# Two key units of the memory moved between the two norms behind the mixing output

## The chip, the cores and the metric

The kernel runs on one core of a Trainium2 chip. TensorE (PE) multiplies into eight PSUM banks, VectorE (DVE), ScalarE (ACT) and GpSimd (POOL) do the elementwise work, SyncE (SP) issues the weight loads. The metric is the device time of one execution in microseconds (us); lower is better. Everything is computed in f32.

## The reference

Two decoder blocks over 256 tokens of width 2048. What matters here is the end of the first block's mixer, its two norms, and the memory attention of the second block:

```python
mix = (gates[..., :D_MODEL] * (o_a @ w_branch_a[l])
       + gates[..., D_MODEL:] * (o_b @ w_branch_b[l])) @ w_out[l]
x = x + _rmsnorm(mix, g_mix_post[l])
h = _rmsnorm(x, g_ffn_pre[l])
gu = h @ w_ffn_in[l]
...
mix = hybrid_mixer(h, ...)            # S5, stick breaking, sparse attention (16 heads)
...
def memory_cross_attention(h, mem, wq, wkv, wo):
    q = (h @ wq).reshape(bsz, t_len, XA_HEADS, XA_HEAD_DIM)
    k, v = jnp.split(mem @ wkv, 2, axis=-1)
```

`mem` (256 x 2048) is an input, so `mem @ wkv` depends on nothing that the kernel computes and can stand anywhere ahead of the memory attention.

## The kernel before

Activations lie transposed, 128 channels by 256 tokens per block, 16 blocks: `xT` (the residual), `hT` and `yT`, 4096 columns each; everything else shares one scratch tile, `arena`. Every projection is cut into **units** of 256 output columns. A unit's 2 MB of weights come through a ring of four slots; `ORDER` is the list of all units, written out by hand, and the SP queue loads them in this order, the load for a slot when the unit four places ahead has been used (`w_used`). The other engines follow programs of their own and meet through semaphores.

There are two kinds of unit. A plain unit (`unit_quarters`, L598) is 32 matmuls of 128x128 by 256 columns, which the trace writes as 64 records; it is a generator that stops after each quarter (8 matmuls), or after each eighth with `step=4`. A "sevens" unit (`unit_sevens`, L550) does seven of eight block products; for these units POOL first adds blocks of the weights (`sum_weights`, four tensor operations, L517 to L522) and DVE combines blocks of the source (L503 to L510). The mixing output ("out") and the first FFN product ("ffn_in") are of this kind.

The memory's projection is four plain units: `mem_k` 0 and 1 (keys), `mem_v` 0 and 1 (values). Before the change `mem_k` 0 runs behind `ffn_out` while the third norm is worked out, reading the memory from `hT`. The other three run beside the 16 heads of the sparse attention (`nsa_pe`), in eighths, reading the memory from `yT`: one eighth ahead of every head's output product and a second one behind it at even heads, 24 in all.

**Between the two norms.** After the eighth unit of "out", PE adds up the squares of that unit (L758, `norm_sum`). ACT takes the root (L735), DVE the reciprocal (L789), multiplies `yT` by it in four chunks (L805, L809) and adds it to `xT` (L811); ACT squares each chunk (L726); PE sums the squares by 16 matmuls (L742, 32 records); then root, reciprocal, and 16 scalings into `hT` (L798). The first product of "ffn_in" waits for `hT` chunk by chunk (L550); its third product waits for the second of DVE's combinations (L506).

**A head** of the sparse attention: six transposes and two small ones (`turn`, from L2208), ACT copies them to SBUF (L2286, L2288), then the output product on PE (L2222 to L2227), ACT copies the result (L2293) and finishes the next head's exponentials (L2269, L2275), DVE normalizes them (up to L2360), and the next head's `turn` may begin. PE computes the scores two heads ahead (L2195 to L2198) as soon as the bank is free, which is after L2293. At heads 4 and 10 POOL does a weight sum for `out2`.

Of the kernel before, what the change touches and what calls it, by code (L numbers as in the profile page):

```python
# [16 lines left out]
T = 256  # L17
# [55 lines left out]

LATE = [("ng", 0), ("nv", 0), ("nv", 1), ("mem_k", 1), ("mem_v", 0), ("mem_v", 1)]
ORDER = [unit for unit in ORDER if unit not in LATE]
_first = ORDER.index(("out2", 0))
# [158 lines left out]
def build(nc, t_in, t_out):  # L235

    ctx = ExitStack()
    with ctx:
# [65 lines left out]
        def stream_weights(sp):  # L304
            for n, home in enumerate(LOADS):
                if n >= RING:
                    sp.wait_ge(w_used, n - RING + 1)
                if isinstance(home, int):
                    sp.dma_start(ring[:, n % RING, :], weights[home, :, :]).then_inc(w_ready[n % RING], 16)
                else:  # L310
                    for half in range(2):
                        q, (a, z) = (home[1] + half) // 3, PAIRS[(home[1] + half) % 3]
                        for row in range(2):
                            to = 2048 * half + 256 * (z - a) * row
                            sp.dma_start(ring[:, n % RING, to:to + 256 * (z - a)],
                                         weights[home[0] + 2 * q + row, :, 256 * a:256 * z])\
                                .then_inc((w_late if half else w_ready)[n % RING], 16)
                if n == UNIT_AT["branch_b0", 0][0] + RING - 1:
                    gate_loads(sp)
                if n == UNIT_AT["mem_k", 1][0]:  # L320
                    nsa_loads(sp)
# [3 lines left out]
        def run(steps):  # L325
            for _ in steps:
                pass
# [378 lines left out]

        NORM_AT = {"mix_post": 0, "ffn_pre": 0}
        POST = {"out": ("norm_units", 0), "ffn_out": ("norm_units", 8), "out2": ("ln_units", 0), "down2": ("ln_units", 8)}

        def norm_space(tag):  # L710
            sq, r = carve(DB * T, T, at=NORM_AT.get(tag, 11264))
            return sq.rearrange("p (b t) -> p b t", b=DB), r

# [30 lines left out]

        def unit_sums(pe, name, src, done):

# [16 lines left out]
            def after(u):  # L763
                released = u // per_slot * per_slot
                for v in range(max(0, released - per_slot), released) if u % per_slot == 0 else ():
                    add(v)
                if u == st.units - 1:
                    for v in range(released, st.units):
                        last = add(v)
                    last.then_inc(sem(done), 1)  # L770
# [776 lines left out]
        bb_combined = combined_in_place(obT, arena[:, 16400:17424], arena[:, 17424:18448], arena[:, 0:1024])  # L1547
        out_combined = combined_in_place(mixT, *carve(1024, 1024, 1024, at=4352))
        out_squares = carve(512, at=7424)[0].rearrange("p (h t) -> p h t", h=2)
        bb_temps = carve(P, T, at=18448)  # L1550
# [21 lines left out]
        def gates_pool(pool):  # L1572
            pool.wait_ge(sem("rw2_Y_sum"), RW_TILES // GT * NCH)
            summed = [("branch_b", u) for u in range(7)] + [("out", u) for u in range(8)]
            for n, (name, u) in enumerate(summed):
# [5 lines left out]
                if n == 4:  # L1581
                    nsa_consts_pool(pool)

        def branch_b_pe(pe):
# [3 lines left out]

        def out_pe(pe):
            short_pe(pe, "out", mixT, lambda u: bb_sums[u % 2], out_combined, "mix_ready", 1,  # L1590
                     unit_sums(pe, "out", out_squares, "norm_sum"))

# [110 lines left out]
        def ffn_dve(dve):  # L1703
# [3 lines left out]
            for u in range(st.units):  # L1707
                left, right, first, u2 = ffn_out_of[u % 2]
                if u == st.units - 1:
                    out_stage_idle(dve, "mem_k")  # L1710
                    sum_weights(dve, "ffn_out", 0, 0, fo_sums[0])
                    group_used(dve, "ffn_in", u - 1, 0)
                    sum_weights(dve, "ffn_out", 0, 1, fo_sums[1])
# [435 lines left out]
        def nsa_pe(pe):  # L2149
# [82 lines left out]
            for h in range(NH):  # L2232
# [3 lines left out]
                if h == 0:  # L2236
                    pe.wait_ge(sem("mem_loaded"), 32)
                next(memory, None)
                output(h)
                if h % 2 == 0:  # L2240
                    next(memory, None)
            run(memory)
            pe.wait_ge(sem("attn_head_done"), NSA_AT_HEAD + NH)

        def nsa_act(act):
# [34 lines left out]
            for h in range(NH):  # L2280
# [13 lines left out]
                if h + 1 < NH:  # L2294
                    exponentials(h + 1, 1)
                if h in (5, 11):
                    store_unit(act, *LATE[3 + h // 6])
            store_unit(act, *LATE[5])

# [377 lines left out]
        def _(pe):  # L2677
# [14 lines left out]
            out_pe(pe)  # L2692
            squares_pe(pe, "ffn_pre", pm[0])
            ffn_pe(pe)
            ffn_out_pe(pe)
            pe.wait_ge(sem("mem_loaded"), 16)
            run(unit_quarters(pe, "mem_k", 0, hT))
            products(pe, "u5", xT, ready="block1_done", count=NCK, chunks=NCK)
# [10 lines left out]
        def _(act):  # L2709
# [16 lines left out]
            root_act(act, "mix_post", pm[0], 0)  # L2726
            squares_act(act, "ffn_pre", xT, "x_mixed", NCK)
            root_act(act, "ffn_pre", pm[0], 0)
            ffn_act(act)
            root_table_act(act)  # L2730
            ffn_out_act(act)
            root_act(act, "ffn_post", pm[0], 0)
            store_unit(act, "mem_k", 0)
            s5_angles_act(act)
# [188 lines left out]
```

## Time and profile before

| | us |
|---|---|
| median of 3 runs | 4033.61 |
| lowest, highest | 4032.55, 4039.31 |
| the profiled execution | 4030.8 |
| its span in the trace | 4028.9 |
| PE busy in it | 3857.7 (96%) |
| POOL busy in it | 1241.4 (31%) |

The span is what the trace covers, from the first to the last instruction. PE is busy almost throughout, so the places that count are those at which PE waits, and those at which it works at a lower granted clock. The profile gives the granted clock as a share of full speed: 1.00 is 2.4 GHz, 0.50 is 1.2 GHz.

### The profile page before, as it was taken

The page shows a single profiled execution, that of the slowest core. Times are in us where ns is not written, and L with a number is a line of the kernel's source. Part 1 is how long each engine was busy: PE and PEld are TensorE (multiplying, and loading weights), DVE is VectorE, ACT ScalarE, POOL GpSimd, SP SyncE. Part 2 cuts the span into 40 slices and gives each one's busy share as a digit, 9 for nine tenths or more (in the row PEclk, how much of TensorE's full clock was granted, in tenths as well). Part 3 has the DMA queues.
Part 4 walks back from the last instruction along what each step waited for, and adds up shares of the span by engine and source line. Part 5 has one row for each costly group of instructions (what it writes and reads, how often), then busy time and mean ns, then how long its engine had stood idle before and what let it go on. Part 6 is the DMA issues. An engine that isn't in the chain of part 4 may idle for free.

```text
span 4028.9 us, 65270 instructions
## 1 busy us (share of the span) xinstructions
PE 3857.7 (96%) x28244; PEld 3561.4 (88%) x28244; DVE 1769.7 (44%) x3203; ACT 600.3 (15%) x1315; POOL 1241.4 (31%) x783
## 2 busy tenths in 40 slices
PE   8999999999999999999999999997798899999997
PEld 7888888888788998999999998776597899999997
DVE  1344425540313513111144455723422688887544
ACT  0333311111111011000000000222302211111001
POOL 0000000003222774777740000001150477775000
PEclk9999999999999999999999999998899999999999
DMA  6566654456654443444444554354142344444442
GB/s 239 195 225 225 220 207 170 160 191 215 194 179 159 155 168 110 170 170 171 170 158 160 172 206 170 140 128 158 45 160 97 115 168 168 168 168 163 167 158 79
DMA packets 109118, 668.81 MB, mean 166 GB/s; under 512 B 23056, under 2 KB 27472, under 8 KB 78496
## 3 DMA queue, kind: packets, MB, share of 16 engines
q1 hardware_dynamic: 64208, 549.01, 37.6%
q0 software_dynamic: 21088, 69.73, 5.8%
q10 hardware_dynamic: 23536, 45.92, 3.2%
q8 instruction: 222, 3.64, 0.4%
q14 instruction: 64, 0.52, 0.0%
HBM read 611.34 MB, written 53.25 MB: 165 GB/s over the span
## 4 chain that ended last, share of the span: by engine, by line
PE 89%; DVE 4%; issue 3%; ACT 2%; POOL 1%; POOLq 1%; DVEq 1%; ACTq 1%; DMA 0%
PE product_bank L550 46%; PE product_bank L598 31%; PE product_bank L392 3%; PE mixer_bank L742 1%; PE mixer_bank L758 1%; POOL arena L519 1%; POOLq L521 1%; POOLq L518 0%; POOL arena L522 0%; ACT xT L859 0%; PE mixer_bank L1271 0%; PE mixer_bank L1285 0%; PE mixer_bank L1122 0%; ACTq L2276 0%; DVE arena L1357 0%
## 5 line engine op out<-in xcount | busy, mean ns | idle before, releaser
L598 PE MATMUL product_bank<-hT,weight_ring 128*128 128x256 f32 x3648 | 812.4, 381 | 0.0
L598 PEld LDWEIGHTS product_bank<-hT,weight_ring 128*128 128x128 f32 x3648 | 689.5, 190 | 103.2 <-issue 10.2
L550 PE MATMUL product_bank<-hT,weight_ring 128*128 128x128 f32 x3680 | 457.6, 277 | 14.1 <-DVEq L1628 5.8
L550 PEld LDWEIGHTS product_bank<-hT,weight_ring 128*128 128x128 f32 x3680 | 435.8, 193 | 16.7 <-issue 6.8
L550 PE MATMUL product_bank<-arena,weight_ring 128*128 128x128 f32 x3200 | 398.5, 275 | 0.0
L550 PEld LDWEIGHTS product_bank<-arena,weight_ring 128*128 128x128 f32 x3200 | 378.5, 192 | 0.6
L517 POOL TENSOR_TENSOR arena<-weight_ring 128x1024 f32<-128x1024 f32 x89 | 212.8, 2391 | 479.5 <-PE product_bank L550 307.7
L574 DVE TENSOR_TENSOR arena<-product_bank,arena 128x128 f32<-128x128 f32 x127 | 36.9, 290 | 730.9 <-PE product_bank L550 730.9
L2601 DVE SCALAR_TENSOR_TENSOR arena<-arena 128x256 f32<-128x256 f32 x176 | 322.4, 1870 | 14.2 <-ACT arena L2566 10.9
L520 POOL TENSOR_TENSOR weight_ring<-weight_ring 128x1024 f32<-128x1024 f32 x111 | 272.1, 2452 | 0.0
L550 PE MATMUL product_bank<-hT,arena 128*128 128x128 f32 x2048 | 250.9, 277 | 0.2 <-DVE hT L506 0.2
L550 PEld LDWEIGHTS product_bank<-hT,arena 128*128 128x128 f32 x2048 | 240.9, 194 | 0.6 <-DVE hT L506 0.6
L519 POOL TENSOR_TENSOR arena<-arena,weight_ring 128x1024 f32<-128x1024 f32 x89 | 212.2, 2385 | 34.2 <-issue 22.6
L522 POOL TENSOR_TENSOR arena<-arena,weight_ring 128x1024 f32<-128x1024 f32 x89 | 212.0, 2382 | 12.9 <-issue 0.4
L550 PE MATMUL product_bank<-yT,weight_ring 128*128 128x128 f32 x1632 | 199.9, 276 | 6.9 <-POOL arena L522 6.9
L550 PE MATMUL product_bank<-yT,arena 128*128 128x128 f32 x1632 | 198.6, 276 | 0.0
L550 PEld LDWEIGHTS product_bank<-yT,weight_ring 128*128 128x128 f32 x1632 | 191.2, 193 | 7.5 <-issue 7.5
L550 PEld LDWEIGHTS product_bank<-yT,arena 128*128 128x128 f32 x1632 | 190.8, 193 | 0.0
L550 PE MATMUL product_bank<-xT,weight_ring 128*128 128x128 f32 x1408 | 174.5, 277 | 8.0 <-ACT xT L859 8.0
L550 PEld LDWEIGHTS product_bank<-xT,weight_ring 128*128 128x128 f32 x1408 | 166.1, 193 | 9.3 <-issue 6.2
L598 PE MATMUL product_bank<-xT,weight_ring 128*128 128x256 f32 x768 | 170.7, 380 | 0.6 <-PE mixer_bank L1941 0.2
L564 ACT ACTIVATE arena<-product_bank 128x128 f32<-128x128 f32 x127 | 34.4, 271 | 875.2 <-PE product_bank L550 864.0
(495 smaller groups left out, 5353.3 us busy)
## 6 DMA issues: line engine op xcount, KB each, us to landing
weight_ring<-in_weights SPq DMA_DIRECT2D x213, 2048.0 KB, 8.0
weight_ring<-in_weights SPq DMA_DIRECT2D x128, 512.0 KB, 5.6
weight_ring<-in_weights SPq DMA_DIRECT2D x64, 384.0 KB, 5.8
units<-out_stage ACTq DMA_DIRECT2D x87, 256.0 KB, 7.8
rwkv_keep<-arena ACTq DMA_DIRECT2D x16, 1282.0 KB, 6.1
arena<-rwkv_keep POOLq DMA_DIRECT2D x8, 1280.0 KB, 7.3
arena<-units POOLq DMA_DIRECT2D x36, 256.0 KB, 3.4
arena<-units POOLq DMA_DIRECT2D x48, 128.0 KB, 6.0
```

Source lines behind the costliest of these rows:

```text
L392: mm = pe.matmul(out, lhs, rhs, start=first, stop=kk == slots * st.blocks - 1, skip_group_check=slots > 1)
L517: eng.tensor_tensor(s1, B11, B12, ALU.add)
L519: eng.tensor_tensor(s2, s1, B22, ALU.add)
L520: eng.tensor_tensor(B12, B12, B22, ALU.add)
L521: eng.drain()
L522: eng.tensor_tensor(s4, s2, B21, ALU.add).then_inc(sem(f"weights_summed_by_{SUMMED_BY[name]}"), 1)
L550: mm = pe.matmul(bank[:, at * P:at * P + P], lhs[:, j, :], rhs[:, j, :], start=g == 0 and n in (0, 3) and j == 0, stop=g == n_groups - 1 a ...
L574: dve.tensor_tensor(u2, X[:, P:2 * P], first, ALU.add)
L598: mm = pe.matmul(psg[b][:, half * T:half * T + T], lhs, rhs, start=k == 0, stop=k == 15)
L742: mm = pe.matmul(bank[:, 0:T], const("ones_mean"), sq[:, b, :], start=b == 0, stop=b == DB - 1)
L758: mm = pe.matmul(pm[0][:, 0:T], const("ones_mean"), v, start=n == 0, stop=n == DB - 1)
L2601: last = dve.scalar_tensor_tensor(V[:, h, :], U[:, h, k:k + T], col(h, k), V[:, h, :], ALU.mult, ALU.add)
```

## The change

Both key units go between the norms. `mem_k` 0 and 1 stand ahead of `ffn_in` in `ORDER`. PE runs one quarter of `mem_k` 0 between the squares' sum of the seventh and of the eighth unit of "out", its three others behind the eighth's, then two quarters of `mem_k` 1, the sum of squares of the second norm, and the last two quarters. POOL loads the memory into `arena` for it (`early_mem`, 2 MB), in its queue behind the weight sum for "out" 1. `mem_v` 0 takes `mem_k` 0's place behind `ffn_out`. Only `mem_v` 1 remains beside the heads, one eighth ahead of the output product of every even head. Scratch places in `arena` move so that nothing overlaps. Around the change only the order and the places differ; the work is the same, but for one more load of the memory.

```diff
-LATE = [("ng", 0), ("nv", 0), ("nv", 1), ("mem_k", 1), ("mem_v", 0), ("mem_v", 1)]
-ORDER = [unit for unit in ORDER if unit not in LATE]
+LATE = [("ng", 0), ("nv", 0), ("nv", 1), ("mem_v", 1)]
+EARLY = [("mem_k", 0), ("mem_k", 1)]
+ORDER = [unit for unit in ORDER if unit not in LATE + EARLY]
+_first = ORDER.index(("ffn_in", 0))
+ORDER[_first:_first] = EARLY
...
                 if u == st.units - 1:
+                    run(filler)
                     for v in range(released, st.units):
                         last = add(v)
                     last.then_inc(sem(done), 1)
...
+                if n == 8:
+                    pool.wait_ge(sem("mix_ready"), 1)
+                    pool.dma_start(early_mem, t_in["memT"]).then_inc(sem("mem_loaded"), 16)
...
         def out_pe(pe):
+            first = unit_quarters(pe, "mem_k", 0, early_mem)
+            def part(n):
+                pe.wait_ge(sem("mem_loaded"), 16)
+                for _ in range(n):
+                    next(first)
+                    yield
             short_pe(pe, "out", mixT, lambda u: bb_sums[u % 2], out_combined, "mix_ready", 1,
-                     unit_sums(pe, "out", out_squares, "norm_sum"))
+                     unit_sums(pe, "out", out_squares, "norm_sum", part(1)))
+            run(first)
+
+        def between_norms_pe(pe):
+            second = unit_quarters(pe, "mem_k", 1, early_mem)
+            next(second)
+            next(second)
+            squares_pe(pe, "ffn_pre", pm[0])
+            run(second)
...
-                next(memory, None)
-                output(h)
                 if h % 2 == 0:
                     next(memory, None)
+                output(h)
             run(memory)
...
-            squares_pe(pe, "ffn_pre", pm[0])
+            between_norms_pe(pe)
             ffn_pe(pe)
             ffn_out_pe(pe)
-            pe.wait_ge(sem("mem_loaded"), 16)
-            run(unit_quarters(pe, "mem_k", 0, hT))
+            pe.wait_ge(sem("mem_loaded"), 32)
+            run(unit_quarters(pe, "mem_v", 0, hT))
...
             squares_act(act, "ffn_pre", xT, "x_mixed", NCK)
+            store_unit(act, "mem_k", 0)
             root_act(act, "ffn_pre", pm[0], 0)
+            store_unit(act, "mem_k", 1)
             ffn_act(act)
```

PE's queue from the end of the last "out" unit to the start of "ffn_in", before (a row is one line of instructions with its count of matmuls; L758 and L742 are the two sums of squares):

```order
L550 MATMUL product_bank<-arena 128x128 x8
L550 MATMUL product_bank<-arena,weight_ring 128x128 x8
L758 MATMUL mixer_bank<-arena,consts 128x256 x4
L742 MATMUL mixer_bank<-arena,consts 128x256 x16
L550 MATMUL product_bank<-hT,weight_ring 128x128 x8
L550 MATMUL product_bank<-hT,arena 128x128 x8
```

and after the change, with the lines moved on by 4 to 7 (L765 and L749 are the sums, L602 is the plain unit):

```order
L554 MATMUL product_bank<-arena 128x128 x8
L554 MATMUL product_bank<-arena,weight_ring 128x128 x8
L765 MATMUL mixer_bank<-arena,consts 128x256 x2
L602 MATMUL product_bank<-arena,weight_ring 128x256 x8
L765 MATMUL mixer_bank<-arena,consts 128x256 x2
L602 MATMUL product_bank<-arena,weight_ring 128x256 x40
L749 MATMUL mixer_bank<-arena,consts 128x256 x16
L602 MATMUL product_bank<-arena,weight_ring 128x256 x16
L554 MATMUL product_bank<-hT,weight_ring 128x128 x8
L554 MATMUL product_bank<-hT,arena 128x128 x8
```

The eighth unit's sum stands behind a quarter of `mem_k` 0; 40 matmuls stand ahead of the second norm's sum and 16 behind it.

PE's queue beside the heads, at the end of an even head's `turn` (L2212), before; L598 is an eighth of a memory unit, L2222 to L2227 the output product, L2195 the scores of the head after next:

```order
L2210 MATMUL mixer_bank<-consts,arena 128x128
L2212 MATMUL mixer_bank<-consts,arena 15x128 x2
L598 MATMUL product_bank<-weight_ring,yT 128x256 x4
L2222 MATMUL mixer_bank<-arena 64x256
L2226 MATMUL mixer_bank<-arena 64x256
L2227 MATMUL mixer_bank<-arena 64x128
L2226 MATMUL mixer_bank<-arena 64x256
L2227 MATMUL mixer_bank<-arena 64x128
L598 MATMUL product_bank<-weight_ring,yT 128x256 x4
L2195 MATMUL mixer_bank<-arena 128x256
L2196 MATMUL mixer_bank<-arena 128x128
L2195 MATMUL mixer_bank<-arena 128x256
```

and after, at an odd head's `turn` (L2240), where the output product is L2250 to L2255 and the scores L2223 and L2224:

```order
L2238 MATMUL mixer_bank<-consts,arena 128x128
L2240 MATMUL mixer_bank<-consts,arena 15x128 x2
L2250 MATMUL mixer_bank<-arena 64x256
L2254 MATMUL mixer_bank<-arena 64x256
L2255 MATMUL mixer_bank<-arena 64x128
L2254 MATMUL mixer_bank<-arena 64x256
L2255 MATMUL mixer_bank<-arena 64x128
L2223 MATMUL mixer_bank<-arena 128x256
L2224 MATMUL mixer_bank<-arena 128x128
L2223 MATMUL mixer_bank<-arena 128x256
```

At even heads the first eighth stays where it was and the second is gone; at odd heads no eighth is left.

## Rows read from the trace of the kernel before

**Rows 1.** windows of core 0 from the last mixing product to the FFN
```profile
core 0: us, PE busy (x) PEld busy (x) DVE busy (x) ACT busy (x) POOL busy (x), PEclk, DMA share, GB/s
1503.30:1514.17 10.87, 2.13 (x10) 1.22 (x8) 8.01 (x10) 3.07 (x5) 5.95 (x3) 0.79 0.51 193
1514.17:1524.16 9.99, 9.95 (x32) 7.97 (x32) 4.81 (x4) 3.17 (x4) 0.00 (x0) 0.72 0.00 0
...
1528.32:1537.05 8.73, 7.72 (x31) 6.83 (x32) 8.45 (x16) 0.00 (x0) 0.00 (x0) 0.51 0.00 0
```

**Rows 2.** timeline of PE there: start us, us, instructions [idle before <-releaser]
```profile
1505.87 1.13 PE L758 MATMUL mixer_bank<-arena,consts 128*128 128x256 f32 x4 [1.57 <-ACT arena L780]
1514.17 9.95 PE L742 MATMUL mixer_bank<-arena,consts 128*128 128x256 f32 x32 [7.17 <-ACT arena L726]
1528.32 1.20 PE L550 MATMUL product_bank<-hT,weight_ring 128*128 128x128 f32 x4 [4.20 <-DVE hT L798]
...
1533.99 3.33 PE L550 MATMUL product_bank<-hT,arena 128*128 128x128 f32 x16
1537.16 1.95 PE L550 MATMUL product_bank<-yT,arena 128*128 128x128 f32 x16
```

**Rows 3.** timeline of ACT and DVE there
```profile
1509.37 1.22 DVE L805 TENSOR_TENSOR yT<-yT,arena 128x1024 f32<-128x1024 f32 x1
...
1519.25 1.06 ACT L726 ACTIVATE arena<-xT 128x1024 f32<-128x1024 f32 x1 [0.26 <-DVE xT L811]
1524.16 0.47 ACT L735 ACTIVATE arena<-mixer_bank,small 128x256 f32<-128x256 f32 x1 [3.86 <-PE mixer_bank L742]
...
1526.50 6.42 DVE L798 SCALAR_TENSOR_TENSOR hT<-xT,params,arena 128x256 f32<-128x256 f32 x16
...
1534.15 1.22 DVE L506 TENSOR_TENSOR yT<-hT 128x1024 f32<-128x1024 f32 x1
```

**Rows 4.** timeline of PE behind the FFN, one whole memory unit
```profile
2370.04 13.98 PE L598 MATMUL product_bank<-hT,weight_ring 128*128 128x256 f32 x64
```

**Rows 5.** timeline of POOL and DVE at the start of the mixing output
```profile
1394.98 3.18 DVE L503 TENSOR_TENSOR arena<-hT 128x1024 f32<-128x1024 f32 x1
1397.22 3.15 POOL L522 TENSOR_TENSOR arena<-arena,weight_ring 128x1024 f32<-128x1024 f32 x1
```

**Rows 6.** DMA issues from 1440 us to 1560 us: count, KB each, median us to landing
```profile
weight_ring<-in_weights SPq DMA_DIRECT2D x7, 2048.0 KB, 7.8
```

**Rows 7.** timeline of the SP queue around the end of "out" 6: start us, us to the last issue
```profile
1490.09 13.70 SPq L309 DMA_DIRECT2D weight_ring<-in_weights  x2
```

**Rows 8.** windows of the heads: all, three intervals, one with a POOL sum; columns as [rows 1]
```profile
2757.67:2928.32 170.65, 133.79 (x648) 100.59 (x648) 86.65 (x345) 60.11 (x231) 32.38 (x34) 0.89 0.20 69
2796.39:2805.80 9.41, 6.77 (x38) 5.10 (x38) 5.02 (x24) 3.90 (x15) 1.06 (x2) 1.00 0.08 21
2805.80:2817.10 11.30, 10.30 (x46) 7.63 (x46) 5.03 (x24) 3.80 (x15) 1.06 (x2) 0.85 0.26 65
...
2826.51:2837.47 10.96, 10.30 (x46) 7.72 (x47) 5.02 (x24) 3.80 (x15) 1.06 (x2) 0.84 0.07 18
...
2769.54:2784.77 15.23, 6.77 (x38) 5.09 (x39) 11.57 (x24) 3.91 (x15) 10.35 (x6) 0.82 0.03 6
```

**Rows 9.** waits of PE beside the heads: us in total, times, longest
```profile
PE mixer_bank L2208 <- DVE arena L2360: 41.2, 16, 8.0
```

**Rows 10.** windows of the heads, the memory units' products alone
```profile
2757.67:2928.32 170.65, 55.35 (x192) 41.76 (x192) 0.89 0.20 69
```

**Rows 11.** timeline of one odd and one even head
```profile
2798.28 0.41 ACT L2288 ACTIVATE arena<-mixer_bank 15x128 f32<-15x128 f32 x2
...
2799.15 0.64 PE L2222 MATMUL mixer_bank<-arena 15*64 15x256 f32 x2
...
2805.80 0.33 PE L2208 MATMUL mixer_bank<-consts,arena 128*128 128x128 f32 x1 [2.17 <-DVE arena L2360]
...
2806.80 3.50 PE L598 MATMUL product_bank<-yT,weight_ring 128*128 128x256 f32 x8
```

More of the change, by code:

```diff
@@ L319, in stream_weights @@
                     gate_loads(sp)
-                if n == UNIT_AT["mem_k", 1][0]:
+                if n == UNIT_AT["mem_v", 1][0]:
                     nsa_loads(sp)
@@ L707, in build @@
         NORM_AT = {"mix_post": 0, "ffn_pre": 0}
+        ROOT_AT = {"mix_post": 17920, "ffn_pre": 17920}
         POST = {"out": ("norm_units", 0), "ffn_out": ("norm_units", 8), "out2": ("ln_units", 0), "down2": ("ln_units", 8)}
@@ L711, in norm_space @@
             sq, r = carve(DB * T, T, at=NORM_AT.get(tag, 11264))
+            if tag in ROOT_AT:
+                r, = carve(T, at=ROOT_AT[tag])
             return sq.rearrange("p (b t) -> p b t", b=DB), r
@@ L743, in squares_pe, with unit_sums @@
             mm.then_inc(sem("norm_sum"), 1)
-        def unit_sums(pe, name, src, done):
+        def unit_sums(pe, name, src, done, filler=()):
             st = PLAN[name]
@@ L1547, in build @@
         bb_combined = combined_in_place(obT, arena[:, 16400:17424], arena[:, 17424:18448], arena[:, 0:1024])
-        out_combined = combined_in_place(mixT, *carve(1024, 1024, 1024, at=4352))
-        out_squares = carve(512, at=7424)[0].rearrange("p (h t) -> p h t", h=2)
+        out_combined = combined_in_place(mixT, *carve(1024, 1024, 1024, at=4096))
+        early_mem = arena[:, 7168:7168 + 4096].rearrange("p (b t) -> p b t", b=DB)
+        out_squares = carve(512, at=17408)[0].rearrange("p (h t) -> p h t", h=2)
         bb_temps = carve(P, T, at=18448)
@@ L1709, in ffn_dve @@
                 if u == st.units - 1:
-                    out_stage_idle(dve, "mem_k")
+                    out_stage_idle(dve, "mem_v")
                     sum_weights(dve, "ffn_out", 0, 0, fo_sums[0])
@@ L2236, in nsa_pe @@
                 if h == 0:
-                    pe.wait_ge(sem("mem_loaded"), 32)
-                next(memory, None)
-                output(h)
+                    pe.wait_ge(sem("mem_loaded"), 48)
                 if h % 2 == 0:
                     next(memory, None)
+                output(h)
             run(memory)
@@ L2295, in nsa_act @@
                     exponentials(h + 1, 1)
-                if h in (5, 11):
-                    store_unit(act, *LATE[3 + h // 6])
-            store_unit(act, *LATE[5])
+            store_unit(act, *LATE[3])
         def nsa_dve(dve):
@@ L2732, in _ @@
             root_act(act, "ffn_post", pm[0], 0)
-            store_unit(act, "mem_k", 0)
+            store_unit(act, "mem_v", 0)
             s5_angles_act(act)
```

## The prediction

> **What bounds the kernel now.** I first read the page: PE is busy 96% of the span, so a move of PE work pays only where it fills a wait of PE or ends a slow clock, and costs where the place it leaves had hidden it. Then the windows and timelines of both places.
>
> Between the norms PE has nothing to do three times: 1.57 us ahead of the eighth unit's sum, 7.17 us ahead of the second norm's, 4.20 us ahead of "ffn_in" [rows 2]. The granted clock goes with it: the sum of squares that follows the long wait gets 0.72 and takes 9.95 us, and "ffn_in" starts at 0.51, which is 1.2 GHz nearly throughout [rows 1]. The reader should see a chain of ACT and DVE (root, reciprocal, multiply, add, square, [rows 3]) that PE waits out. This place can swallow work.
>
> Beside the heads PE waits too, 41.2 us over 16 heads, always for DVE's last normalization [rows 9], though 24 eighths of memory units, 55.35 us of PE, lie there [rows 10]. So the eighths don't bound the heads, but the loop PE, ACT, PE, ACT, DVE does. An odd interval (an eighth ahead of the output, none behind) takes 9.41 us at clock 1.00; an even one, with two eighths, 11.30 or 10.96 us at 0.85 or 0.84 [rows 8]. Where does the difference come from? The second eighth runs while ACT and DVE work, and DVE releases the odd `turn` behind it too (16 of 16). The difference is the clock: ahead of the even `turn` PE idles 2.17 us, and right behind it the eighth takes 3.50 us for 8 records [rows 11], against 13.98 / 8 = 1.75 us by the whole unit [rows 4]. 1.75 of the 1.89 us difference is this one eighth.
>
> **The change, part by part.**
>
> *PE between the norms.* A quarter of a unit is 13.98 / 4 = 3.5 us at full clock [rows 4]. The seventh unit's sum starts at 1503.3 and takes about 0.9 us. Then:
> - the first quarter ends at 1507.6, and the eighth unit's sum starts there and not at 1505.87 [rows 2]: the norm chain is 1.75 us late, and the last square (1519.25 + 1.06 = 1520.3 before, [rows 3]) at 1522.1;
> - sum to 1508.5, five quarters, 17.5 us, to 1526.0;
> - the second norm's sum, 32 records, costs two quarters' worth at full clock, 7.0 us, to 1533.0, instead of 1524.1;
> - the last two quarters to 1540.0. Meanwhile root, reciprocal and scalings: before, from L735 at 1524.16 to the end of L798 at 1532.92 are 8.8 us, and to the end of L506 at 1535.37 are 11.2 us [rows 3]. So `hT` is whole at 1541.8 and the third product of "ffn_in" may start at 1544.2. It started at 1537.16 [rows 2], held by the slow clock (the second product took 3.33 us).
>
> That makes +7.0 us for 28.0 us of work: 21 us are hidden. PE is late by its own work up to 1540, then DVE for 2 us.
>
> *POOL and SP.* Two loads now stand ahead of "ffn_in" in the SP queue, so the weights for "ffn_in" 0 are asked for when "out" 6 is done (1490) and for 1 when "out" 7 is (1503), the two issues of [rows 7], and land 7.8 us later [rows 6]. POOL sums them, some 10.35 us each [rows 8], from about 1498 and 1511, needed at 1540 and later: no wait. But the second sum now runs on top of DVE's ten-odd us of norm work. Where the two engines met before, DVE's L503 took 3.18 us beside a POOL operation of 3.15 us [rows 5]; the same shape alone takes 1.22 us [rows 3]. Four POOL operations cost DVE about 4 x 2.0 = 8 us: the last square comes at 1530.1, and PE wants it at 1526.0 + 3/4 of 7.0 = 1531.3. So I take 0, with 1.2 us to spare: the cover is `mem_k`'s quarters. Without that cover it is up to +8.
>
> The Trainium skill, page GPSIMD Engine Reference, section 1. Specifications, has this as a rule against the change: GpSimd's SBUF interfaces are shared with VectorE, with contention for DVE instructions with two SBUF inputs, as L805 to L811 are. The trace agrees (3.18 against 1.22 us). By that rule alone nothing of the sum changes while the cover holds.
>
> *The other queues.* POOL's load of the memory waits for `mix_ready` behind the sum for "out" 1, which ends at 1400.4 [rows 5]; behind it stands the sum for "out" 2, which waits for PE anyway. 100 us lie before its use. ACT's two copies of `mem_k` are one activation each, under the 1.06 us of L726 [rows 3], behind which the second root waits for PE. "mem_v" 0 costs behind the FFN what `mem_k` 0 did [rows 4]. All 0. Lower bound for the whole place +6 (DVE's last 2 us overlap better), upper +12 (half of the contention uncovered).
>
> *The heads.* 16 eighths go, 16/24 of 55.35 = 37 us of PE. At odd heads the output may start when ACT's copies are done (2798.28 + 0.41 = 2798.7) and not at 2799.15 [rows 11]: -0.4 us, at six of eight, since at two the POOL sum sets the pace (15.23 us, POOL 10.35, [rows 8]): -2. At even heads the eighth behind the output was hidden: 0. What is left is the clock. The eighth that filled the time ahead of every odd `turn` is gone, so that PE now idles over 2 us ahead of every `turn`, not of every second one. Bounds from rows: never a fall of the clock, even intervals 9.41 instead of 11.30 or 10.96 us, eight times -1.6, with the -2 makes -15. A fall at every head: odd intervals lose what their output product loses at half clock, at most the 1.75 us of an eighth (nearly as many columns), so about +1.3 net at six, +8, and +12 if it outlasts one head. Falls as often as now: -2. A wait that makes the clock fall at even heads should do so at some odd heads, not all, since an even interval lost 1.89 us and another 1.55 [rows 8], and heads differ: I take the middle of -2 and +10, **+4**.
>
> The Trainium skill, page TensorE: Matmul & The Clock Gate, section What's actually happening, says that the throttled state is the default and activity releases it. By that a thinner stage is slower: the case of +8 to +12. The trace agrees in kind: the intervals at 1.00 are those that follow the filled wait [rows 8].
>
> *Sum.* Against the profiled execution's 4030.8 us (span 4028.9): +7 + 4 = 4042. The median of the runs is 2.8 us above it, so 4033.6 + 11 = **4045**.
>
> **The rivals.** Differences under 0.2%, 8.1 us, can't be told from none here.
> 1. *Forecast*: norms +7, heads 0 to +12: 4041 to 4053. Chance 0.53.
> 2. *The clock falls beside the heads as often as now*: 7 - 2, 4039. For it: one fall a pair is regular; against: the waits double. 0.20.
> 3. *The clock stays up beside the heads*: 7 - 15, 4026, just within 0.2%. Against: every long wait of [rows 11] is followed by a slow stretch. 0.08.
> 4. *The heads shorten by what leaves them* (the other side): if the eighths sat on the loop, -37, so 4033.6 + 7 - 37 = 4004. It decides once the heads give back over 15 us (7 + 8.1), and wants the output product and `turn` to wait for PE's own queue; [rows 9] show DVE as releaser 16 times of 16. 0.05.
> 5. *Contention uncovered*: both POOL sums on the norm chain, twice 8 us against 9.2 us of cover, so about +7 more with the heads at +4: 4052. 0.14.
>
> **How the numbers follow.** Likeliest 4045. Range 4034 to 4056: it leaves out 3 and 4 (0.13) and the far tail of 5 and of slow heads. The forecast's own range is 4041 to 4053. Slower by over 0.2% (from 4041.7): most of 1, all of 5: 0.64. Within: the rest of 1, 2, most of 3: 0.29. Faster: 4 and a bit of 3: 0.07.
>
> **What would show it.** In the profile after: PE busy without a wait from the last "out" product to "ffn_in", clock 1.00 there; the second norm's sum about 7 us long; "ffn_in"'s third product 40 to 42 us after the seventh unit's sum (34 before); DVE multiplications of over 3 us instead of 1.22. Beside the heads: odd intervals with clock below 1.00, the 16 heads 170.65 + 4 us, PE's waits up from 41 to 70 us or more. Wrong if odd intervals keep 1.00 (then 2 or 3), or if PE waits for a square (then 5).

## The result: 0.6% slower, and outside the range

| | before | after |
|---|---|---|
| median, us | 4033.08 (4 runs) | 4060.32 (4 runs) |
| lowest, highest | 4031.74, 4039.31 | 4058.56, 4063.30 |
| the profiled execution | 4030.8 | 4061.84 |
| heads, first `turn` to the first product of "out2" | 171.9 | 191.0 |

The ratio is 1.0063, 95% interval 1.0047 to 1.0079. The forecast was 4045, with a range up to 4056: the sign was right, the size was not. The page of the changed kernel, its span and PE's busy time:

```profile
span 4060.0 us, 65273 instructions
PE 3884.3 (96%) x28244; PEld 3578.2 (88%) x28244; DVE 1775.4 (44%) x3203; ACT 600.1 (15%) x1315; POOL 1244.7 (31%) x784
```

PE has the same 28244 records as before, yet is busy 26.6 us longer (3857.7 before). The same matmuls took longer, so the clock comes first, and waits second. I laid the two PE timelines over each other, instruction by instruction, and noted by how much the changed kernel was behind. This gives four steps:

| place | behind by | grown there |
|---|---|---|
| third product of "ffn_in" | 6.9 us | +6.9 |
| `turn` of the first head | 9.1 us | +2.2 |
| first product of "out2" | 28.1 us | +19.1 |
| behind "out2", in the memory attention | 31.2 us | +3.1 |

The two spans differ by 31.1 us (4060.0 - 4028.9), so nothing is missing. (The difference of the medians is 27.2: the profiled execution of after was 1.5 us above its median, that of before 2.3 below.)

**Between the norms** everything is as forecast. PE's timeline of the changed kernel:

```profile
1504.06 3.62 PE L602 MATMUL product_bank<-arena,weight_ring 128*128 128x256 f32 x16
1507.51 1.03 PE L765 MATMUL mixer_bank<-arena,consts 128*128 128x256 f32 x4
1508.38 17.43 PE L602 MATMUL product_bank<-arena,weight_ring 128*128 128x256 f32 x80
1525.64 7.07 PE L749 MATMUL mixer_bank<-arena,consts 128*128 128x256 f32 x32
1532.55 7.07 PE L602 MATMUL product_bank<-arena,weight_ring 128*128 128x256 f32 x32
1539.46 1.50 PE L554 MATMUL product_bank<-hT,weight_ring 128*128 128x128 f32 x12
1541.57 0.71 PE L554 MATMUL product_bank<-hT,weight_ring 128*128 128x128 f32 x4 [0.61 <-DVE hT L806]
...
1544.02 1.16 PE L554 MATMUL product_bank<-yT,arena 128*128 128x128 f32 x8
```

Against [rows 2] the three waits (1.57, 7.17, 4.20 us) are gone, the second norm's sum takes 7.07 us instead of 9.95, and one wait of 0.61 us for `hT` is left. The third product starts 6.9 us later (1537.16 before); the sum had +7.0. On the timelines of DVE and POOL the contention is there, and PE does not see it:

```profile
1512.06 3.37 DVE L817 TENSOR_TENSOR yT<-yT,arena 128x1024 f32<-128x1024 f32 x1
1515.51 3.22 DVE L819 TENSOR_TENSOR xT<-xT,yT 128x1024 f32<-128x1024 f32 x1
...
1511.14 3.21 POOL L521 TENSOR_TENSOR arena<-weight_ring 128x1024 f32<-128x1024 f32 x1 [3.72 <-DMA weight_ring<-in_weights]
...
1529.10 1.06 ACT L733 ACTIVATE arena<-xT 128x1024 f32<-128x1024 f32 x1 [0.26 <-DVE xT L819]
```

**Beside the heads** the windows of the changed kernel (columns as [rows 1]; the whole stretch, an odd and an even interval in its first half, an odd and an even one in its second):

```profile
2766.73:2957.69 190.96, 137.74 (x520) 95.90 (x521) 84.11 (x346) 59.88 (x231) 32.42 (x34) 0.67 0.13 45
2830.09:2841.50 11.41, 7.49 (x30) 4.79 (x31) 5.03 (x24) 3.91 (x15) 1.06 (x2) 0.66 0.07 19
2841.50:2853.65 12.15, 9.64 (x39) 6.95 (x39) 5.02 (x24) 3.80 (x15) 1.06 (x2) 0.75 0.07 16
...
2879.07:2890.74 11.67, 9.42 (x30) 6.46 (x30) 5.03 (x24) 3.91 (x15) 1.06 (x2) 0.50 0.07 18
2890.74:2902.22 11.48, 8.97 (x39) 6.82 (x39) 5.02 (x24) 3.80 (x15) 1.06 (x2) 0.80 0.06 17
```

In an odd interval DVE, ACT and POOL are busy as long as in [rows 8] (5.03, 3.91 and 1.06 us against 5.02, 3.90 and 1.06). What changed is the clock: 0.67 over the stretch instead of 0.89, and 0.50, which is 1.2 GHz from end to end, in the odd intervals of the second half, but for the last head. PE has 128 fewer records there than before (520 against 648) and is busy longer, 137.7 us against 133.8. Its waits:

```profile
PE mixer_bank L2236 <- DVE arena L2385: 42.9, 16, 7.6
PE mixer_bank L2250 <- ACTq L2316: 10.2, 8, 1.3
PE mixer_bank L2223 <- ACT hT L2320: 6.5, 14, 0.5
```

The wait for DVE hardly grew (41.2 in [rows 9]; the prediction looked for 70 or more), since slow PE work now fills the time in which fast PE work would have left it idle. New is the second row: with no eighth ahead of it, the odd output product waits for ACT's copies. One such odd head on PE's timeline:

```profile
2879.07 0.47 PE L2236 MATMUL mixer_bank<-consts,arena 128*128 128x128 f32 x1 [2.41 <-DVE arena L2385]
...
2882.32 1.11 PE L2250 MATMUL mixer_bank<-arena 15*64 15x256 f32 x2 [1.27 <-ACTq L2316]
2883.36 1.12 PE L2254 MATMUL mixer_bank<-arena 128*64 128x256 f32 x2
...
2886.65 1.22 PE L2223 MATMUL mixer_bank<-arena 64*128 64x256 f32 x2 [0.47 <-ACT hT L2320]
```

From `turn` to the output product are 3.25 us, against 2.76 in [rows 11] (2796.39 to 2799.15), where an eighth lay in between. From the start of the output product to ACT's copy of it (L2320) are 3.90 us, against 2.13 before, and from there to the next `turn` 4.52 us in both. The transposes, the output product and the scores all run at half speed, and the first two are on the loop.

### The profile page after: what moved, and what is told of

It reads as the page before. It is cut to its first block, busy times and chain, and to the rows that moved or that the text cites. A ratio compares the mean times of both kernels' runs of the same rounds, so it can differ in the third digit from the quotient of the medians.

```text
span 4060.0 us, 65273 instructions
## 1 busy us (share of the span) xinstructions
PE 3884.3 (96%) x28244; PEld 3578.2 (88%) x28244; DVE 1775.4 (44%) x3203; ACT 600.1 (15%) x1315; POOL 1244.7 (31%) x784
## 4 chain that ended last, share of the span: by engine, by line
PE 89%; DVE 3%; issue 3%; ACT 2%; POOL 1%; POOLq 1%; DVEq 1%; ACTq 1%; DMA 0%
PE product_bank L554 45%; PE product_bank L602 31%; PE product_bank L396 3%; PE mixer_bank L749 1%; PE mixer_bank L765 1%; POOL arena L523 1%; POOLq L525 1%; POOLq L522 0%; POOL arena L526 0%; ACT xT L867 0%; PE mixer_bank L2254 0%; PE mixer_bank L1279 0%; PE mixer_bank L1293 0%; PE mixer_bank L1130 0%; ACTq L2303 0%
## 5 line engine op out<-in xcount | busy, mean ns | idle before, releaser
L602 PE MATMUL product_bank<-hT,weight_ring 128*128 128x256 f32 x3584 | 798.4, 381 | 0.0
L602 PEld LDWEIGHTS product_bank<-hT,weight_ring 128*128 128x128 f32 x3584 | 677.3, 190 | 101.5 <-issue 10.2
L554 PEld LDWEIGHTS product_bank<-hT,weight_ring 128*128 128x128 f32 x3680 | 435.2, 193 | 12.7 <-DVEq L1656 6.0
L554 PEld LDWEIGHTS product_bank<-xT,weight_ring 128*128 128x128 f32 x1408 | 166.2, 193 | 9.3 <-issue 6.2
L602 PE MATMUL product_bank<-xT,weight_ring 128*128 128x256 f32 x768 | 172.4, 383 | 0.6
L602 PEld LDWEIGHTS product_bank<-xT,weight_ring 128*128 128x128 f32 x768 | 146.2, 192 | 22.3 <-issue 2.1
```

The costliest lines, as they stand in the source:

```text
L554: mm = pe.matmul(bank[:, at * P:at * P + P], lhs[:, j, :], rhs[:, j, :], start=g == 0 and n in (0, 3) and j == 0, stop=g == n_groups - 1 a ...
L602: mm = pe.matmul(psg[b][:, half * T:half * T + T], lhs, rhs, start=k == 0, stop=k == 15)
```

## The experiments

None of the kernels leaves out work. "Idle" matmuls are added work whose result nobody reads. A "group" is four matmuls of 128x128 by 256 columns, an eighth of a memory unit or idle work of that size. The table orders the kernels by their groups beside the heads; "heads" is the time from the first `turn` to the first product of "out2" in the profiled execution. Each ratio is to runs of the kernel before that were taken together with the kernel's own, whose medians were 4032.0 to 4033.8 us.

| kernel | groups ahead of / behind the output | heads, us | median, us | ratio to before |
|---|---|---|---|---|
| after | 8 / 0 | 191.0 | 4060.3 | 1.0063 |
| `e8_pool_later` | 8 / 0 | 191.0 | 4059.7 | 1.0067 |
| `e7_idle_ahead` | 16 / 0 | 187.2 | 4059.6 | 1.0061 |
| `e10_half_idle` | 8 and 8 half / 8 half | 178.6 | 4051.8 | 1.0048 |
| `e4_one_between` | 0 / 16 | 176.9 | 4038.9 | 1.0012 |
| before | 16 / 8 | 171.9 | 4033.1 | |
| `e1_idle_as_before` | 16 / 8 | 171.9 | 4042.8 | 1.0025 |
| `e2_idle_behind` | 8 / 16 | 172.3 | 4044.0 | 1.0024 |
| `e3_behind` | 8 / 16 | 173.4 | 4035.4 | 1.0003 |
| `e5_filled` | 16 / 16 | 166.0 | 4029.2 | 0.9986 |
| `e6_filled_norms` | 16 / 16, and idle work between the norms | 166.6 | 4030.7 | 0.9993 |
| `e9_filled_long` | 16 / 16 and long waits | 162.5 | 4025.3 | 0.9975 |

**Idle work in the old places.** My theory after the result: the 19 us are the clock, and the clock fell because work was taken from PE.

```diff
+            def idle_work():
+                for k in range(4):
+                    pe.matmul(psg[(spare + 1) % 4][:, 0:T], xT[:, k, 0:P], yT[:, k, :], start=k == 0, stop=k == 3)
...
                 if h % 2 == 0:
                     next(memory, None)
+                else:
+                    idle_work()
                 output(h)
+                if h % 2 == 0:
+                    idle_work()
```

> The changed kernel with idle matmuls beside the sparse attention's heads: four matmuls of 128x128 by 256 columns, as long as an eighth of a memory unit, into a product bank whose contents nobody reads, at each of the 16 places where the kernel before had an eighth and the changed one has none (ahead of the output at odd heads, behind it at even ones). They add computation and no loads. Theory A, the 19 us that the heads grew by are the lower clock and nothing else of the move: with PE's old load back the 16 heads take 171 us again instead of 191, the granted clock there is back near 0.89, PE's waits for DVE are back near 41 us, and the total is 4033 + 7 (norms) + 2 (the stretch ahead of the heads) = 4042, though PE does 37 us more of work than in the changed kernel. Theory B, the heads grew for another reason (their exponentials, the weight loads or POOL's sums now fall elsewhere): the total stays at 4060 and the heads at 190 us. Theory C, work on PE is what bounds the heads: the added 37 us make it slower, up to 4097.

4042.84 us, ratio 1.0025 (1.0015 to 1.0034). The windows of the heads, of an odd and of an even one:

```profile
2766.44:2938.32 171.88, 133.77 (x648) 100.60 (x649) 87.52 (x346) 59.95 (x231) 32.39 (x34) 0.89 0.15 51
2805.17:2814.58 9.41, 6.77 (x38) 5.10 (x38) 5.02 (x24) 3.91 (x15) 1.06 (x2) 1.00 0.08 21
2814.58:2825.89 11.31, 10.30 (x47) 7.62 (x47) 5.03 (x24) 3.80 (x15) 1.06 (x2) 0.85 0.08 20
```

The two intervals are those of [rows 8] again, to 0.01 us, and the stretch takes the 171.9 us of the kernel before. PE got 16 groups of work that is good for nothing, and the median fell by 17.5 us from that of the changed kernel (4060.3). Theory A holds; loads, POOL and DVE's contention have no part in the 19 us.

**Does the place of a group matter?** Three kernels ask it from different sides. First the changed kernel with the idle groups behind the output at every head:

```diff
                 output(h)
+                idle_work()
```

> The changed kernel with the same idle group of four matmuls behind the output product of every head, odd ones too, and none ahead of it; the eighth of the value unit stays ahead of the output at even heads. The same 16 groups as in the kernel with idle work at the old places, but eight of them stand where PE waits for DVE and not where ACT and DVE wait for PE. Theory A, the clock follows how long PE stands still ahead of each turn: with an eighth behind every output no wait is over 1 us, the granted clock stays at 1.00, odd and even intervals take 9.4 us as the odd ones of the kernel before, the heads come to about 155 us, and the total to 4060 - 36 = 4025. Theory B, the clock follows only how much work there is in all, not its place: as with the old places, 4042. Theory C, the place behind the output is no cover, since DVE's normalization is done by then: each head grows by up to 1.75 us, above 4060.

Second the kernel before with its own eighths in that order:

```diff
-                next(memory, None)
-                output(h)
                 if h % 2 == 0:
                     next(memory, None)
+                output(h)
+                next(memory, None)
```

> The kernel before, with its 24 eighths of memory units in another order beside the heads: behind the output product at every head, and ahead of it only at even heads (before: ahead of it at every head, behind it only at even ones). Everything else, the norms too, is as before. Theory A (waits ahead of turn set the clock): all intervals at 9.4 us, heads 155 us instead of 171, total 4033 - 16 = 4017. Theory B (only the amount of PE work counts): no difference from the kernel before, 4033 within 4 us.

4044.0 (1.0024, 1.0013 to 1.0034) and 4035.4 (1.0003, 0.9993 to 1.0012): both theories A are wrong. With 24 groups the order makes no difference to the total that can be measured, though it changes which intervals are slow. Windows of the heads of `e3_behind`, and of three intervals, two odd ones with an even one behind the second:

```profile
2757.89:2931.24 173.35, 143.49 (x648) 103.71 (x649) 89.29 (x348) 61.16 (x233) 32.38 (x34) 0.85 0.18 65
...
2816.09:2825.12 9.03, 6.97 (x38) 5.09 (x38) 5.03 (x24) 4.51 (x16) 1.06 (x2) 1.00 0.55 228
2859.32:2870.60 11.28, 10.00 (x38) 6.82 (x39) 4.98 (x23) 3.92 (x15) 1.06 (x2) 0.70 0.06 18
2870.60:2879.88 9.28, 8.63 (x48) 6.53 (x47) 5.19 (x24) 3.80 (x15) 1.06 (x2) 1.00 0.64 233
```

and the two odd heads on PE's timeline, the first in the interval at 1.00 and the second in the one at 0.70:

```profile
2816.09 0.33 PE L2208 MATMUL mixer_bank<-consts,arena 128*128 128x128 f32 x1 [1.00 <-DVE arena L2360]
2818.46 0.64 PE L2222 MATMUL mixer_bank<-arena 15*64 15x256 f32 x2 [1.28 <-ACTq L2289]
...
2859.32 0.33 PE L2208 MATMUL mixer_bank<-consts,arena 128*128 128x128 f32 x1 [1.01 <-DVE arena L2360]
2861.70 1.11 PE L2222 MATMUL mixer_bank<-arena 15*64 15x256 f32 x2 [1.28 <-ACTq L2289]
```

Both have the same two waits; in the one the output product ran at full clock (0.64 us), in the other at half (1.11 us). So waits of 1.0 and 1.3 us can be enough for a fall, and need not be. At full clock and with no eighth ahead of it, the output product starts 2.37 us behind `turn`, and the interval is 9.03 us instead of 9.41.

Third the changed kernel with idle groups ahead of the output at odd heads alone:

```diff
                 if h % 2 == 0:
                     next(memory, None)
+                else:
+                    idle_work()
                 output(h)
```

> The changed kernel with 8 idle groups beside the heads, all ahead of the output product of odd heads, so that one eighth or its like stands ahead of every output and none behind: half of what the change took away. Theory A (the wait of over 2 us ahead of a turn brings the slow stretch; filling only the far side of the output leaves a 2.17 us wait ahead of every turn): heads stay above 185 us, total 4056 or more. Theory B (the clock follows the amount of work in the heads, in proportion): halfway between 171 and 191, so heads 181 us and total 4050. Theory C (one group a head is enough, as it was with the groups behind the output): heads 172 us, total 4042.

4059.55 us (1.0061), heads 187.2 us: the times are theory A's, and B and C are out. PE still stands still for 2.04 us or more ahead of every `turn`. Sixteen groups all ahead of the output give 187.2 us, sixteen all behind it (`e4_one_between`, below) 176.9. So the place matters, below 24 groups. The windows of the heads, first of `e7_idle_ahead`, then of `e4_one_between`, show that it doesn't act through the share of slow time:

```profile
2766.96:2954.17 187.21, 136.80 (x584) 101.13 (x585) 84.91 (x346) 59.89 (x231) 32.41 (x34) 0.78 0.13 47
...
2758.44:2935.35 176.91, 138.57 (x584) 95.42 (x585) 89.99 (x348) 60.55 (x232) 32.39 (x34) 0.78 0.15 51
```

The mean clock is 0.78 in both. What differs is what runs slowly. In `e7_idle_ahead` the group ahead of the output is on the loop at half clock, and from `turn` to the output product are 4.1 to 5.3 us at every head; in `e4_one_between` 2.37 us, or 3.25 where `turn` itself is slow.

**A third arrangement of the same work.** One key unit between the norms, the other back beside the heads, an eighth behind each output (the diff is against the changed kernel).

```diff
-LATE = [("ng", 0), ("nv", 0), ("nv", 1), ("mem_v", 1)]
-EARLY = [("mem_k", 0), ("mem_k", 1)]
+LATE = [("ng", 0), ("nv", 0), ("nv", 1), ("mem_k", 1), ("mem_v", 1)]
+EARLY = [("mem_k", 0)]
...
-            run(first)
+            next(first)
+            next(first)
+            squares_pe(pe, "ffn_pre", pm[0])
+            run(first)
...
-                if h % 2 == 0:
-                    next(memory, None)
                 output(h)
+                next(memory, None)
```

> The same work as before and after, in a third arrangement: only the first key unit between the norms (one quarter between the two sums of squares of the mixing output, two ahead of the second norm's sum, one behind it), the second key unit and the second value unit beside the heads with one eighth behind the output product of every head and none ahead, the first value unit behind the FFN. Theory A (one hidden eighth per head keeps the clock up): heads 155 to 158 us, the norms within 2 us of the kernel before, total 4033 - 15 = 4018. Theory B (16 eighths are too few for the clock wherever they stand): heads at 180 us or more, total 4040 or more. Theory C (the clock stays at the old share): 171 us, total 4032.

4038.9 us (1.0012, 1.0002 to 1.0021), heads 176.9 us: none of the three; the total is nearest to B's. PE's timeline between the norms:

```profile
1503.88 1.03 PE L765 MATMUL mixer_bank<-arena,consts 128*128 128x256 f32 x4
1504.74 3.62 PE L602 MATMUL product_bank<-arena,weight_ring 128*128 128x256 f32 x16
...
1509.06 7.07 PE L602 MATMUL product_bank<-arena,weight_ring 128*128 128x256 f32 x32
...
1537.80 1.96 PE L554 MATMUL product_bank<-yT,arena 128*128 128x128 f32 x16
```

From the seventh unit's sum to the third product are 33.9 us, as in [rows 2] (1503.3 to 1537.16) without any of `mem_k` there. The first unit between the norms is free there, and the second one costs the 7 us. But even the free place gains nothing: the heads, with 16 groups left, took 5.0 us more than before.

**Filling the heads.** Now the kernel before with an idle group behind odd outputs too, so that only waits of 0.65 to 1.0 us are left ahead of most `turn`s.

```diff
                 output(h)
                 if h % 2 == 0:
                     next(memory, None)
+                else:
+                    idle_work()
```

> The kernel before with an idle group of four matmuls (128x128 by 256 columns, a result that nobody reads) behind the output product of every odd head, so that an eighth or its like stands ahead of and behind every output: 32 instead of 24. It adds 8 x 1.75 = 14 us of PE work and changes nothing else. Theory A (a slow stretch needs a wait of some length on PE; the ones that were left when the eighths stood behind every output were 1.28 us ahead of odd outputs and 1.0 ahead of turns, and that was still enough): here only the waits of 0.65 to 1.0 us ahead of turn are left, the granted clock stays at 1.00, intervals are 9.4 to 9.6 us, the heads take 157 us instead of 171, and the total is 4032 - 14 = 4018. Theory B (the slow stretch comes once in two heads whatever stands there, as in the four kernels with 16 or 24 groups): heads 171 us, total 4032. Theory C (the added work lengthens the loop): above 4035.

4029.24 us, ratio 0.9986 (0.9978 to 0.9995): 14 us more of PE work, and faster. The windows of the heads, an odd and an even one:

```profile
2759.68:2925.64 165.96, 142.06 (x713) 107.32 (x714) 88.03 (x347) 61.49 (x234) 32.41 (x34) 0.92 0.21 73
2798.46:2807.88 9.42, 8.63 (x47) 6.54 (x47) 5.04 (x24) 3.91 (x15) 1.06 (x2) 1.00 0.08 21
2807.88:2817.50 9.62, 8.62 (x47) 6.53 (x47) 5.03 (x24) 3.80 (x15) 1.06 (x2) 1.00 0.29 70
```

Theory A in direction, under half of it by size (5.9 of 14 us in the heads): five even intervals fell from 10.8 to 11.3 us to 9.3 to 9.6, which is 8.2 us, but the last head took 2.2 us more. I had counted eight. Whether it was the shorter waits or the larger amount of work that kept the clock up, this kernel can't tell, since it changes both; `e3_behind` had waits of 1.0 us too, with less work, and lost the clock behind some of them.

Then the long waits as well:

```diff
+                for k in range({0: 16, 2: 13, 8: 9}.get(h, 0)):
...
+                    pe.matmul(psg[(spare + 1) % 4][:, 0:T], xT[:, k % 4, 0:P], yT[:, k % 4, :], start=True, stop=True)
                 turn(h)
```

> The kernel with 32 groups beside the heads (24 eighths of memory units and 8 idle groups, which ran in 4029), with idle matmuls also in the three long waits that were left there: 16 ahead of the first head's turn, 13 ahead of the third's, 9 ahead of the ninth's (0.44 us each at full clock, in waits of 7.6, 6.6 and 4.8 us). Theory A (a slow stretch follows a long wait, and costs up to 2 us an interval): the intervals behind them fall from 11.9, 11.6 and 11.3 us to 9.4 to 9.6, those with a POOL sum stay at 13.4 to 15.2, which POOL sets; the heads take 160 us instead of 166, total 4029 - 6 = 4023. Theory B (these intervals are slow because POOL's sum slows DVE in them, not by PE's clock): no change, 4029.

4025.32 us, ratio 0.9975 (0.9966 to 0.9984), 8.5 us below the kernel before in the runs taken with it (4033.8): the fastest of all. The windows of its heads and of the first three intervals:

```profile
2758.66:2921.20 162.54, 147.34 (x756) 111.84 (x757) 89.29 (x347) 61.42 (x234) 32.43 (x34) 0.98 0.21 75
2758.66:2768.30 9.64, 8.62 (x47) 6.53 (x47) 5.04 (x24) 3.80 (x15) 1.06 (x2) 1.00 1.00 423
2768.30:2784.70 16.40, 14.43 (x73) 11.39 (x73) 12.84 (x24) 3.91 (x15) 10.37 (x6) 1.00 0.03 9
2784.70:2793.97 9.27, 8.62 (x46) 6.53 (x47) 5.02 (x24) 3.80 (x15) 1.06 (x2) 1.00 0.13 36
```

Theory A, and B is out: 11.9 us became 9.64 and 11.6 became 9.27, and the ninth interval, not shown, 9.65 instead of 11.30. But the interval with POOL's sum took 16.40 instead of 15.24, and the tenth one fell to 0.85 and took 1.7 us more, so 3.4 of the 6 us came.

**Half the amount.** The first experiment again, with

```diff
-                for k in range(4):
+                for k in range(2):
```

> The changed kernel with idle groups at the 16 old places of the eighths, as in the run that took 4043, but of two matmuls instead of four: half of the PE work that the change took from the heads. Theory A (with so much the slow stretch still ends in time, since a group stands on both sides of each output): heads 175 us or less, total 4046 or less. Theory B (in proportion to the work): heads 181 us, total 4051. Theory C (half-filled waits count as unfilled): heads 187 us or more, total 4056 or more.

4051.84 us (1.0048), heads 178.6 us: between A and B by the heads. Half of the work gives back 12.4 of the 19.1 us there.

**Contention.**

```diff
                 if u == 1:
+                    pool.wait_ge(sem("norm_squares"), SQUARES_AT["ffn_pre"] + NCK)
                 sum_weights(pool, "ffn_in", u, 0, ffn_sums[u % 2])
```

> The changed kernel, in which POOL's weight sum for the second unit of the first FFN product waits until ACT has squared the last chunk of the second norm. In the changed kernel that sum runs on top of DVE's four norm operations, which take 3.2 to 3.4 us each instead of 1.22. Theory A (the prediction's: contention is covered by the quarters of the second key unit): DVE's operations take 1.22 us again, the last square comes near 1522 instead of 1530, PE does not notice, and the total is 4060 within 2 us. Theory B (part of the 7 us lost between the norms, or of the 27 us in all, is this contention, for instance through hT, which is needed at 1540): up to 4 us faster, 4056. Theory C (the sum comes too late for its unit): slower, by up to 6 us, with a wait of PE for POOL.

4059.72 us (1.0067): theory A. DVE and ACT in this kernel:

```profile
1513.73 1.22 DVE L817 TENSOR_TENSOR yT<-yT,arena 128x1024 f32<-128x1024 f32 x1
1515.03 1.23 DVE L819 TENSOR_TENSOR xT<-xT,yT 128x1024 f32<-128x1024 f32 x1
...
1522.47 1.06 ACT L733 ACTIVATE arena<-xT 128x1024 f32<-128x1024 f32 x1 [0.26 <-DVE xT L819]
```

The last square starts at 1522.47 instead of 1529.10, though the whole place began 1.7 us later in this execution, and nothing comes of it: from the seventh unit's sum to the third product of "ffn_in" are 40.83 us in both kernels. The cover was real.

**Filling the norms.** The kernel before with its heads filled, and 3, 14 and 10 idle products of constants in the three waits of [rows 2].

```diff
+        def norm_idle(pe, n):
+            for _ in range(n):
+                pe.matmul(pm[1][:, 0:T], const("ones_mean"), consts[:, 0:T], start=True, stop=True)
...
+            norm_idle(pe, 14)
             squares_pe(pe, "ffn_pre", pm[0])
+            norm_idle(pe, 10)
```

> As the kernel with 32 groups beside the heads, and idle matmuls between the two norms as well: products of constants into a bank of PSUM that nobody reads there, 3 ahead of the eighth unit's sum of squares, 14 ahead of the second norm's sum, 10 ahead of the first FFN product (each 0.44 us at full clock; PE waits 1.57, 7.17 and 4.20 us there in the kernel before). Theory A: the granted clock there is 1.00, the second norm's sum takes 7 us and not 9.95, ends 2 us earlier, the first FFN products run at full clock behind it, and the third product starts 4 us earlier than in the kernel before, so the total is 4 us below that of the kernel with the heads filled alone. Theory B: the chain of DVE and ACT sets the time there, not PE's clock: no difference, within 1 us.

4030.74 us (0.9993, 0.9984 to 1.0002), no faster than with the heads alone. The third product did start 3.0 us earlier than before (1534.13 against 1537.16), nearly as theory A has it. In the profiled execution the gain was given back from 550 us later on, at three places. PE's timeline at one place of the second block, first in the kernel before,

```profile
2534.49 0.70 PE L2012 MATMUL mixer_bank<-arena,consts 128*128 128x256 f32 x2 [2.17 <-DVEq L2058]
```

then here:

```profile
2533.18 1.20 PE L2018 MATMUL mixer_bank<-arena,consts 128*128 128x256 f32 x2 [2.17 <-DVEq L2064]
```

and in the changed kernel and `e10_half_idle`, which have the same program for PE up to the heads:

```profile
2541.45 0.70 PE L2040 MATMUL mixer_bank<-arena,consts 128*128 128x256 f32 x2 [2.17 <-DVEq L2086]
...
2543.81 1.22 PE L2040 MATMUL mixer_bank<-arena,consts 128*128 128x256 f32 x2 [2.17 <-DVEq L2086]
```

The same product behind the same wait of 2.17 us ran at full clock before and at half here. It cost 0.5 us on this row and 1.7 us by 2537. A wait of 2.00 us at 2088 had cost 1.6 us in the same way, and one of 3.02 us at 2672 cost 1.7 more, so the first `turn` was 2.2 us late instead of 3.0 early. Did the idle work between the norms cause that? It isn't shown. None of the three places fell in the kernel before, `e3_behind`, `e5_filled` or `e9_filled_long`, but the last two rows show that one program can go both ways: all three fell in the execution of `e10_half_idle`, only the third in that of the changed kernel, and none in that of `e1_idle_as_before`.

## Why the prediction was wrong

*Norms, +7.0: right*, 6.9 measured, with its parts (sum 7.07 us, DVE 3.2 to 3.4 us, PE late by its own work, then for `hT`, though it stood still for 0.61 us and not for 2).

*Contention 0: right*, shown by `e8_pool_later`; the last square came at 1530.2 where 1530.1 was worked out.

*Heads, +4: the step that failed.* It measured +19.1, and all of it is the clock, by `e1_idle_as_before`. The mechanism was named (PE idles ahead of every `turn`, and the clock falls); what failed is the price of a fall.
- "A fall at every head: odd intervals lose ... at most the 1.75 us of an eighth, so about +1.3 net." Measured at the six: 2.0 us at two and at the last head, 2.25 at three, 12.8 together, where the sum had 8. The 1.75 us were right: up to ACT's copy of it, the output product took 3.90 us instead of 2.13, 1.77 more. The 0.4 us booked for an output product that no longer waits behind an eighth are real too, at full clock (2.37 us behind `turn` instead of 2.76, in `e3_behind`). What the sum put at nothing is `turn` itself: with its transposes at half clock the output product starts 3.25 us behind it and not 2.37, 0.88 more. 1.77 + 0.88 - 0.39 is 2.26. I took the cost of a fall from a row where the fall lay on a filler; once the filler is gone, it lies on `turn`, the output product and the scores.
- Even intervals were to lose nothing more. They lost 0.1 to 1.2 us, 5.7 together, since `turn` there starts at half clock as well (up to 5.31 us from `turn` to the output product, 4.43 before).
- The two odd intervals with a sum on POOL, which were to lose nothing, lost 0.6 together.

Then I took the middle of my bounds (-2 and +10), where the runs lie beyond even the +12 of a fall that outlasts one head. The Trainium skill, page TensorE: Matmul & The Clock Gate, section What's actually happening, has the throttled state as the default, which activity releases. The trace agrees in kind: half of a head pair ran at 0.50 once the work had gone, and came back when idle work stood in its place.

*The rest, +5.3, was not in the sum.* 2.2 us came ahead of the heads, 1.7 us of it at one place near 2680: behind the same wait of 3.02 us, a run of 32 records of a plain unit's products took 7.07 us before and 8.76 us after. That isn't the change's: in `e1_idle_as_before`, with the same program up to there and the same wait, it took 7.07 us again. 3.1 us came at "out2", most of it where PE waits for POOL:

```profile
3000.50 3.22 PE L554 MATMUL product_bank<-hT,weight_ring 128*128 128x128 f32 x16 [3.33 <-POOL arena L526]
```

Before, this wait was 1.86 us and the product took 2.02. POOL stood 7.61 us ahead of its second operation there, 6.14 before. What in this is the later start and what the loads was not tried; in `e1_idle_as_before` the same wait is 2.7 us, and the product behind it takes 2.02 us again.

## What to carry to other kernels

Work of PE that hides in a stage bound by other engines may also be what keeps that stage's clock up. Before moving it out, ask what the critical matmuls cost at half clock, all of them, and not what the moved work costs. A place with idle time takes work for free only up to its idle time (here 14 of 28 us), and a move from one place where the work is free to another gains nothing; it can lose what the work did for the clock. Where a stage keeps PE idle a fifth of the time, idle matmuls in its waits can pay: here 8.5 us.

## What the runs showed that I had not expected

- **The half clock can last.** In the changed kernel, odd intervals ran at 0.50 from end to end, though PE was busy 9.42 of 11.67 us in them.
- **The same wait need not have the same effect.** Behind 2.17 us at 2534 the clock stayed in one kernel and fell in another; behind 1.00 and 1.28 us beside the heads it did both in one kernel. So two executions can differ by 1.7 us a place with no edit behind it (the changed kernel and `e10_half_idle` at 2541), and a difference of that size in a single trace proves nothing. The Trainium skill, page TensorE: Matmul & The Clock Gate, section What's actually happening, says that the monitor which sets the clock runs freely and does not start with the kernel; by that, the moment at which a wait falls would decide. The runs agree as far as the same wait did both, even in one program, but none of them tested it.
- **Contention is two-sided.** DVE's operations of 1.22 us took 3.2 to 3.4 us beside POOL's, and POOL's 2.35 us took 3.15 to 3.34.
